# Adding a residual in groups of four tiles, and summing pairs of squares on GpSimd before TensorE's sum, in a two-block network kernel

## What is computed

```python
def rms_norm(v, g):
    vf = v.astype(F32)
    y = vf * lax.rsqrt(jnp.mean(vf * vf, axis=-1, keepdims=True) + RMS_EPS)
    return (y * g.astype(F32)).astype(v.dtype)
```

## Time and profile before

| | |
|---|---|
| median of 3 runs | 3307.74 (3307.04 to 3309.56) |
| profiled execution | 3307.34 |
| its span, first to last instruction | 3305.7 |
| TensorE busy | 3227.1 (98%) |
| VectorE busy | 2204.6 (67%) |
| ScalarE busy | 1241.4 (38%) |
| GpSimd busy | 196.2 (6%) |

### The profile page before, as it was taken

The page is one execution under the profiler, slowest core; times in us unless marked ns, Lnnn a source line. Parts: engine busy times, 40 slices in busy tenths (PEclk is TensorE's granted clock), DMA queues, the critical chain, the costliest instruction groups (busy, mean ns, idle before and its releaser), DMA issues.

```text
span 3305.7 us, 58756 instructions
## 1 busy us (share of the span) xinstructions
PE 3227.1 (98%) x23408; PEld 2700.4 (82%) x23408; DVE 2204.6 (67%) x3396; ACT 1241.4 (38%) x1686; POOL 196.2 (6%) x298
## 2 busy tenths in 40 slices
PE   7999999999999999989999999989999999999998
PEld 4764685478888999978888888878888888888887
DVE  2377656665655677667878777787666667667667
ACT  2202130144444421344344444444544443443444
POOL 0000000012122000000000000000000000000000
PEclk9999999999999999999999999999999999999999
DMA  9956727622222688637767777745445557656654
GB/s 408 364 204 229 277 86 258 241 84 89 89 92 98 234 353 349 228 140 258 276 244 271 256 256 259 255 169 180 161 153 178 191 190 261 210 190 241 225 179 156
DMA packets 101013, 709.02 MB, mean 214 GB/s; under 512 B 11200, under 2 KB 11328, under 8 KB 19520
## 3 DMA queue, kind: packets, MB, share of 16 engines
q1 hardware_dynamic: 73872, 525.89, 43.9%
q0 software_dynamic: 23184, 169.88, 13.9%
q10 hardware_dynamic: 3744, 10.23, 0.8%
HBM read 698.36 MB, written 7.60 MB: 214 GB/s over the span
## 4 chain that ended last, share of the span: by engine, by line
PE 92%; DVE 4%; DMA 2%; issue 1%; ACT 1%; DVEq 0%; SPq 0%; ACTq 0%; POOLq 0%
PE ps L2704 33%; PE ps L2703 17%; PE ps L632 11%; PE ps L2407 3%; PE ps L1099 3%; PE ps L399 2%; PE ps L2700 2%; PE ps L1819 2%; PE ps L1100 2%; PE ps L1101 2%; PE ps L1833 1%; PE ps L2389 1%; PE ps L2388 1%; PE ps L2390 1%; PE ps L1091 1%; PE ps L2701 1%
## 5 line engine op out<-in xcount | busy, mean ns | idle before, releaser
L2704 PE MATMUL ps<-hT_parts,rows_parts 128*128 128x512 f32 x3210 | 1130.6, 394 | 0.0
L2703 PE MATMUL ps<-hT_parts,ring_parts 128*128 128x256 f32 x3210 | 901.9, 281 | 1.7 <-DVE hT_parts L2676 1.6
L2667 DVE TENSOR_TENSOR ring_parts<-ring,rows_parts 128x2048 fp32r<-128x2048 f32 (+1 forms) x337 | 762.1, 2262 | 102.7 <-ACT rows_parts L2662 101.7
L2662 ACT ACTIVATE rows_parts<-ring 128x2048 fp32r<-128x2048 f32 (+1 forms) x337 | 639.4, 1897 | 406.2 <-DMA ring<-in_mlp_u 209.1
L2704 PEld LDWEIGHTS ps<-hT_parts,rows_parts 128*128 128x128 f32 x3210 | 604.2, 188 | 125.0
L2703 PEld LDWEIGHTS ps<-hT_parts,ring_parts 128*128 128x128 f32 x3210 | 607.9, 189 | 12.6 <-DVE hT_parts L2676 2.9
L2704 PE MATMUL ps<-work_parts,rows_parts 128*128 128x512 f32 x1616 | 570.1, 395 | 0.0
L2703 PE MATMUL ps<-work_parts,ring_parts 128*128 128x256 f32 x1616 | 454.2, 281 | 0.0
L632 PE MATMUL ps<-hT,ring 128*128 128x512 f32 (+1 forms) x1088 | 372.4, 505 | 0.0
L2704 PEld LDWEIGHTS ps<-work_parts,rows_parts 128*128 128x128 f32 x1616 | 304.2, 188 | 63.2
L632 PEld LDWEIGHTS ps<-hT,ring 128*128 128x128 f32 x1088 | 206.9, 190 | 163.4 <-issue 152.0
(11 more groups left out here) (495 smaller groups left out, 4532.5 us busy)
## 6 DMA issues: line engine op xcount, KB each, us to landing
ring<-in_mlp_u SPq DMA_DIRECT2D x128, 1024.0 KB, 5.0
ring<-in_ffn_u SPq DMA_DIRECT2D x88, 1024.0 KB, 4.8
rows<-in_mod_r POOLq DMA_DIRECT2D x64, 1024.0 KB, 5.2
ring<-in_gate_u SPq DMA_DIRECT2D x64, 1024.0 KB, 5.2
work<-in_ada_r POOLq DMA_DIRECT2D x64, 1024.0 KB, 5.2
ring<-in_in_u SPq DMA_DIRECT2D x36, 1024.0 KB, 4.8
rows<-in_ada_r POOLq DMA_DIRECT2D x32, 1024.0 KB, 9.0
ring<-in_down_u SPq DMA_DIRECT2D x32, 1024.0 KB, 4.9
```

The lines of the kernel that those rows point to most:

```text
L2662: act.activation(unit_high(u)[:, 0:size], slot(u)[:, 0:size], ACT.Copy).then_inc(hi_done, 1)
L2667: dve.tensor_tensor(ring_parts[:, ring_slot(u), 0:size], slot(u)[:, 0:size], unit_high(u)[:, 0:size].bitcast(F32), ALU.subtract)\
L2703: pe.matmul(ps[:, b, low_half], low, top(kt), start=False, stop=False)
L2704: mm = pe.matmul(ps[:, b, :], high, both(kt), start=False, stop=kt == kts - 1)
```

## The change

`add_scaled` works on groups of four tiles. ScalarE multiplies each tile of y by its gain beforehand, in place (`scale_tile`, counted on `merge_sum`): in `Mix` in the loop over the units, behind the tile's square; in `Mlp` after the last unit, two tiles before the small root and fourteen behind it. VectorE then does four multiplies of 128x1024 by the spread rows and adds of 128x1024 (the last group in two halves of 128x512), and `nadd` rises by 4 or 2 at a time. GpSimd adds the two squares of each of the first seven pairs (128x256, in place), and TensorE's wide sum takes the seven pair sums and then the two squares of the last pair. `pool_done`, used by the earlier stage up to `PAIR_SUMS`, counts the pair sums. In GpSimd's queue the sums of the first turn stand ahead of the memset, those of the second behind the last row DMAs of `Mlp`.

```diff
@@ class Rms
+        PAIR_SUMS = 4 * len(ROUNDS)
-            def __init__(self, src, ready, summed=0, reset=1, last=None, turns=1):
+            def __init__(self, src, ready, summed=0, reset=1, last=None, turns=1, turn=None):
...
-                    for kt in range(KT):
-                        if kt % self.step == 0:
-                            pe.wait_ge(nsq, self.first + kt // self.step + 1)
+                    for kt in (*range(0, KT - 2, 2), KT - 2, KT - 1):
+                        if kt < KT - 2:
+                            pe.wait_ge(pool_done, PAIR_SUMS + (NPAIR - 1) * self.turn + kt // 2 + 1)
+                        else:
+                            pe.wait_ge(nsq, self.first + NPAIR)
                         mm = pe.matmul(ps[:, self.use[0], 0:T], kc("ones"), self.squares[:, kt, :], start=kt == 0, stop=kt == KT - 1)
...
+            def gpsimd(self, pool, own):
+
+                assert own.n == PAIR_SUMS + (NPAIR - 1) * self.turn
+                for n in range(NPAIR - 1):
+                    pool.wait_ge(nsq, self.first + n + 1)
+                    own.step(pool.tensor_tensor(self.squares[:, 2 * n, :], self.squares[:, 2 * n, :], self.squares[:, 2 * n + 1, :], ALU.add))
...
-        def add_scaled(dve, own, src, col, rms):
-
-            for kt in range(KT + 1):
-                if kt < KT:
-                    own.step(dve.tensor_tensor(src[:, kt, :], src[:, kt, :], rms.rows, ALU.mult))
-                if kt:
-                    own.settle(1 if kt < KT else 0)
-                    t = kt - 1
-                    dve.scalar_tensor_tensor(xT[:, t, :], src[:, t, :], col[:, t:t + 1], xT[:, t, :], ALU.mult, ALU.add).then_inc(nadd, 1)
+        def scale_tile(act, y, gain):
+
+            act.activation(y, y, ACT.Copy, scale=gain).then_inc(merge_sum, 1)
+
+        def add_scaled(dve, own, src, rms, scaled):
+
+            for g in range(KT // 4 + 1):
+                if g < KT // 4:
+                    group = src[:, 4 * g:4 * g + 4, :]
+                    dve.wait_ge(merge_sum, scaled + 4 * (g + 1))
+                    own.step(dve.tensor_tensor(group, group, bc(rms.rows, 4), ALU.mult))
+                if g:
+                    own.settle(1 if g < KT // 4 else 0)
+                    size = 4 if g < KT // 4 else 2
+                    for t in range(4 * (g - 1), 4 * g, size):
+                        dve.tensor_tensor(xT[:, t:t + size, :], xT[:, t:t + size, :], src[:, t:t + size, :], ALU.add).then_inc(nadd, size)
             rms.read(dve)
@@ Mix.scalar, in the loop over the units
-                        rms_y1.square_out(act, yT1[:, bass.ds(it * 4 + j, 1), :], sq1[:, bass.ds(it * 4 + j, 1), :])
+                        t = bass.ds(it * 4 + j, 1)
+                        rms_y1.square_out(act, yT1[:, t, :], sq1[:, t, :])
+                        scale_tile(act, yT1[:, t, :], gn1[:, t])
@@ Mix.vector
-                add_scaled(dve, own, yT1, gn1, rms_y1)
+                add_scaled(dve, own, yT1, rms_y1, 2 * PAIRS2)
                 rest_unit(dve, seg_mlp + AHEAD_DVE)
@@ Mlp.scalar, after the loop
+                for t in range(2):
+                    scale_tile(act, yT2[:, t, :], gn3[:, t:t + 1])
                 rms_y2.scalar(act)
+                for t in range(2, KT):
+                    scale_tile(act, yT2[:, t, :], gn3[:, t:t + 1])
@@ Mlp.gpsimd
+                rms_x1.gpsimd(pool, own)
                 pool.wait_ge(nadd, KT)
                 pool.memset(flat(yT2), 0.0).then_inc(pool_tiles, 1)
                 pool.wait_ge(x_split, KT)
                 fetch_late(pool, 0, LATE_ROWS)
+                rms_x2.gpsimd(pool, own)
@@ Mlp.vector
-                add_scaled(dve, own, yT2, gn3, rms_y2)
+                add_scaled(dve, own, yT2, rms_y2, 2 * PAIRS2 + KT)
```

More of the change, by code:

```diff
@@ L2543, in __init__ @@
                 squares_done[0] += summed if summed else KT // self.step
-                self.added, self.last = sums_added[0], last
+                self.added, self.last, self.turn = sums_added[0], last, turn
                 if summed:
@@ L2761, in branch_kernel @@
         assert SQ0 + 3 * T <= WORK - T - SMALL2_N
-        rms_x1 = Rms(xT[:, :, :], lambda e, n: e.wait_ge(nadd, 2 * n + 2))
+        rms_x1 = Rms(xT[:, :, :], lambda e, n: e.wait_ge(nadd, 2 * n + 2), turn=0)
         smallw2 = w(WORK - T - SMALL2_N, SMALL2_N)
@@ L2937, in branch_kernel @@
         assert CONSTS["strict0"][0] + D + 2 * T <= CONSTS["pool_inv"][0]
-        rms_x2 = Rms(xT[:, :, :], lambda e, n: e.wait_ge(nadd, KT + 2 * n + 2))
+        rms_x2 = Rms(xT[:, :, :], lambda e, n: e.wait_ge(nadd, KT + 2 * n + 2), turn=1)
         def small2(name):
```

## The result

The changed kernel takes 3313.73 us (median of 22 runs, 3308.91 to 3318.38) against 3309.51 (22 runs, 3305.02 to 3313.51): a ratio of 1.0013, 95% interval 1.0007 to 1.0018. That is 4.2 us more, small but clear of the noise of 22 runs; it is within the 0.2% named in the prediction. The interval alone reaches from 2.3 to 6.0 us. The profiled execution took 3313.20, its span is 3311.5 (before: 3305.7).

A forecast was written before the change was run, and what follows sets the result against it. TensorE, busy 98% of the span, bounds the kernel; VectorE sets the two turns the change touches. First turn +3.3 and second +0.9 give +4.2, on the median of 3307.74 a forecast of 3311.9, range 3306.0 to 3315.0.

The forecast's parts named there:

- the 0.2% named in the prediction: Whole kernel: 6.6 us, about what a measurement can tell from no change; chance 0.85 of landing within it.
- The absolute forecast: Whole kernel: +4.2 on the median of 3307.74, giving 3311.9.
- VectorE's part and the blocking: Both turns: grouped adds alone take 9.2 against 11.72, but VectorE's adds and GpSimd's sums take turns, holding 0.55 per GpSimd operation.
- `rest_unit` before sum 7: First turn: VectorE's 2.30-long `rest_unit` is served first, so the seventh pair sum ends at 13.9; second turn 12.2.
- Half clock at the end of the sum: Three last products cost 3.0 at half clock, 1.65 at full; root +3.3 in the first turn, +0.9 in the second.
- the sign of being right: Both turns: the root comes 2 to 3.3 later in the first and 0.3 to 1.6 later in the second.
- The twin products, taken as 0: After the root: a low clock could lose 0.5 more per turn or up to 1.7, a missed one gains; taken as 0.
- A sign of being wrong: First turn: a `rest_unit` itself lengthened to 2.8 behind the seventh pair sum.
- Rival (c): Both turns: TensorE's clock stays low through sum and twin products; price 6.9, or 0.7 more, 3314.6 to 3315.4; chance 0.13.
- Rival (a): Both turns: VectorE and GpSimd do not take turns; together -2.0 to +0.6, 3305.7 to 3308.3; chance 0.10.
- Rival (b): Both turns: GpSimd's sums are ready before square 8; root at 11.5, -2.1 per turn, 3303.5; chance 0.02.
- ScalarE's scales: Gains multiplied by ScalarE, 0.49 each, costed at nothing, 0.4 each if uncovered; second turn's first square waits 0.2.

The follow-up runs named there:

- e9: Changed kernel, but TensorE sums all sixteen squares; GpSimd's seven sums go where nothing reads them, only VectorE waits for them; ratio to the kernel before 1.0000.
- e1: Changed kernel without GpSimd's pair sums: grouped adds and ScalarE's scales stay, TensorE sums all sixteen squares; ratio to the kernel before 1.0000.
- e3: Changed kernel with one more wait: in the first turn VectorE begins `rest_unit` only after GpSimd's seventh sum; ratio to the kernel before 1.0005.
- e4: Changed kernel with ten extra TensorE products ahead of the real sum in both turns, their result overwritten; ratio to the kernel before 1.0008.
- e5: Changed kernel with TensorE taking the last pair's two squares ahead of GpSimd's seventh sum; ratio to the kernel before 1.0011.
- e6: e1 plus extra TensorE products, seven ahead of the sum and eight ahead of the twin products; ratio to the kernel before 0.9991.
- e8: e6 with every group of four added in two halves and five extra products instead of seven ahead of the sum; ratio to the kernel before 0.9991.
- e7: Kernel before with only eight extra products between the wide sum and the first twin product in both turns; ratio to the kernel before 0.9998.
- e2: GpSimd's pair sums alone: adds tile by tile as in the kernel before, no scales on ScalarE; ratio to the kernel before 1.0021.

## Why the prediction was right

The median came out 4.2 above before, the sum that was forecast. The mechanism was right: the turns between VectorE and GpSimd, `rest_unit` ahead of sum 7 and three products at half clock are all in the rows. That the number agrees to a tenth is luck. The terms as they measured in the profiled execution, 3.6 and 1.0 at the roots and 0.5 and 0.6 in the twin products, add up to 5.7, and the interval of the 22 runs reaches from 2.3 to 6.0. The absolute forecast, 3311.9, was 1.8 too low: it stood on a median of 3 runs of the kernel before, 3307.74, where 22 runs gave 3309.51.

- **VectorE's part and the blocking.** Computed last square 11.34, measured 11.52. The hold of 0.55 read from the earlier trace rows gave a1 a delay of 0.25; it is 1.50 long instead of 1.22. e9 shows the same rows with TensorE's dependence taken out, e1 without the sums.
- **`rest_unit` before sum 7.** Computed end of sum 7 at 13.9, measured 14.17; second turn computed 12.2, measured 12.43. e3 shows the mechanism by undoing it, at 12.12.
- **Half clock at the end of the sum.** First turn computed 16.9, measured 17.20, which is 3.6 later than before and so 0.3 beyond the 2 to 3.3 that was named as the sign of being right. The two prices of the three last products, 1.65 at full clock and 3.0 at half, are both met: 1.65 (e4, second turn) and 3.03. Second turn: range 13.9 to 15.2 with 14.5 taken, measured 14.63; the clock did come back near the end of its products (0.81 granted over 2215 to 2218). e5 shows that the products behind the seventh sum count, e4's second turn that their clock does.
- **The twin products, taken as 0, were too cheap.** They cost 0.5 and 0.6 more in the profiled execution, because the clock fell before they began and was low for their first 4.4 and 4.9 us (before: for 3.4 and 2.9 of them). In e3 and e5 they take 13.4 to 13.7, in e6 to e8 12.2 to 12.3. I had given the bound (0.5 to 1.7 each) but not used it.
- **A sign of being wrong that needs an answer.** The prediction named a `rest_unit` lengthened to 2.8 behind sum 7. It did last 2.81, but behind sum 6: it ended at 13.6, ahead of sum 7 at 14.17, as the schedule had it.
- **Not foreseen:** in the first turn the clock was already low when the spread products of the small norm ran, 1.19 instead of 0.68 long. They end before t = 0, so this is no part of the 5.6 above. Where the fall lands differs between executions of the same code: at t = 1.6 in the kernel before and at -0.5 in e7, which differ in nothing up to there.
- **Rival (c), low clock throughout,** is what the first turn of the profiled execution shows, from the sum to the twin products, at +4.0; the second turn didn't follow it. Its argument that the clock needs 5.7 of unbroken products doesn't hold as a fixed price: in the second turn of the kernel before it came back 4.5 after the sum's first product. Rival (a), no blocking, fell with the first add of 1.50. Rival (b), sums ready before square 8, fell with the end of sum 7, 14.17 against 11.52.
- **ScalarE's scales** cost about what was assumed: nothing in the first turn, where the sixteenth ends before the small root can start. In the second the fourteen end at 3.9, the first square begins at 3.8 instead of 3.5, and the last square ends at 11.79 instead of 11.52.

## What to carry to other kernels

An instruction moved to GpSimd is not free because GpSimd is idle. Look at what VectorE runs at that moment: where both read two SBUF operands, they took turns here, and one long VectorE instruction that nobody needs yet can hold back the short sum that everybody waits for. Let the long one wait, or let TensorE sum what comes.

Work taken from TensorE next to a stretch of waiting can cost time. In these turns the root came between 12.1 and 14.7 after sixteen products that waited for ScalarE's squares alone, and between 14.1 and 17.2 after nine that waited for GpSimd's sums. Two things make the difference in the first turn: the wait for the last sum (2.2) and the half clock of the products behind it (1.4).

## What the runs showed of the hardware

- VectorE and GpSimd alternate instruction by instruction when both read two SBUF operands: a 128x1024 add goes from 1.22 to 1.50 or 1.77, a 128x512 add from 0.69 to 1.21, a 128x256 scaled add from 0.48 to 0.77, and a 128x256 GpSimd sum from 0.72 to 2.77 behind a 128x2048 operation. VectorE's multiplies with a PSUM operand stayed at 1.21.
- TensorE's granted clock fell to half in a stretch of work with gaps (1.40 busy in 3.00), at t = 11.9 in e4, and stayed at 1.00 through the same pattern of work in that kernel's second turn. It came back after 5.7 of unbroken products in the first turn before and after 4.5 in the second. After 2.93 unbroken it came back in e2's second turn, 0.2 behind the last of them, and did not in its first nor in the first turn of the changed kernel. So one trace of one kernel doesn't tell when the clock changes.
- Three products of 128x256 behind the last sum took 1.65 up to the root at full clock and 3.03 at half.
- Two turns of one and the same kernel differ by 1.25 at the root (e1: 12.86 and 14.11) with their last squares within 0.01; what differs is when the clock returns, 7.1 and 9.6. It may be part of the spread of some 8 us between runs of one kernel; no run here shows how much.
